# Hybrid pooling and chunked attention block: four half products between two attention tiles move into the heads, the sums of squares move from the heads to between the tiles

## The chip, the cores and the metric

The kernel runs on one core of one Trainium2 chip. The metric is the device time of one execution in microseconds (us), less is better; the times below are from three runs, with their median. Engines are named as the profile names them: PE is TensorE, which multiplies matrices, PEld its weight loads, DVE is VectorE, ACT is ScalarE, POOL is GpSimd, and SP is SyncE, which issues the DMAs.

## What is computed

One layer for 4096 rows of width 1024. The rows are normalised and projected to 3072 columns: a value and a gate for a pooling mixer, and q, k, v and a gate for attention with 8 heads of width 64. Attention goes by chunks of 64 rows; each chunk reads itself and the 8 chunks before it, with a bias by clipped distance. The core of the reference:

```python
def one_chunk(args):
    c, qb = args
    start = c * CHUNK
    kb = lax.dynamic_slice_in_dim(kp, start, BAND, axis=1)
    vb = lax.dynamic_slice_in_dim(vp, start, BAND, axis=1)
    s = jnp.einsum('bqhd,bkhd->bhqk', qb, kb).astype(jnp.float32) * scale + bias[None]
    valid = (start + j - pad) >= 0
    s = jnp.where(valid[None, None, None, :], s, MASK_VALUE)
    p = jax.nn.softmax(s, axis=-1)
    return jnp.einsum('bhqk,bkhd->bqhd', p.astype(vb.dtype), vb)
...
y_attn = chunked_rel_attention(qh, kh, vh, rel_bias[layer]) * jax.nn.silu(attn_g)
y = jnp.concatenate([y_pool, y_attn], axis=-1)
x = x + jnp.einsum('bse,ed->bsd', y, w_out[layer])
...
return rms_norm(x, final_norm_gain)
```

## The kernel before

Three stages follow one another: the normalised rows with the values and gates (until about 450 us), the pooling mixer with its share of the output (until about 890 us), and attention, which is what the change is in. Numbers that need more than 16 bits are kept as a high and a low f16 part.

Attention goes over 16 tiles `t` of 256 queries (`ATILES`, the last is `LAST`). Every engine has its own program, in the order in which it is written, and waits on semaphores. Each tile is a `boundary(t)` followed by `heads(t)`, eight heads `h`.

In the heads, PE makes the scores of head `h` in three groups `k` = 0, 1, 2 (`scores`, L1677 to L1685), in two banks that alternate; the scores two groups later may begin when the exponential has read the bank. Group 1 is the biased one: DVE adds the bias (`add_bias`, L1913) before ACT takes the exponential. ACT makes for each group the exponential (L1808) and its high half (L1814), POOL the low half (`p_lo`, L2029), and PE multiplies the values with both (`values(t, h - 1)`, L1705 to L1707), behind the scores of head `h`. Two heads ahead, PE makes the scores once more in the other layout (`maxima`, L1647, two per head, in one pair of banks) and DVE takes the row maximum with the bias (`maximum`, L1899); PE turns the maxima to rows (`max_rows`, L1659) and ACT copies them beside the queries (`max_row`, L1792). The next maxima wait for the DVE operation before them.

Meanwhile PE makes K and Q of tile `t + 1`, as seven products each by a scheme of the Strassen kind: K is w = 2t + 2, Q is w = 2t + 3. Each product is two halves of 12 matmuls (`kq_half`, L1489 to L1492), so a tile has 28 halves. Products 0 and 4 are copied by ACT (`kq_copy_p1` L1503, `kq_copy_c11` L1509), products 1, 2, 3, 5 and 6 are taken by DVE (`kq_take` 0 to 4, L1526). Product 0 of Q waits for all five takes of K. When K is complete, ACT makes its high half (`kq_hi`, L1534, at `K_HI_AT`) and POOL its low half (`kq_lo`, L1538, behind the `p_lo` of the head that `K_HI_AT` names). Take 2 of Q, of product 3, writes over the sums that `kq_lo` reads, and waits for it. DMAs from SP then move K and Q into place; the first maxima of a tile wait for them.

A table by hand, `KQ_SLOTS`, says how many halves stand in each head behind the scores of group 0 and of group 1; `KQ_BEFORE` says how many stand in `boundary`. The output product of tile `t - 1` (`output`, L1623) is in heads 6 and 7 and in the next boundary, its sum with the residual rows on DVE (`residual`, L1943). The mean of squares of the finished rows of tile `t - 2` is made by ACT (`square`, L1823), its root by POOL (`rstd`, L2037, L2039, in heads 1 and 2), and the rows are scaled by DVE (`finish`, L1952, at the end of heads 2 and 3).

## Time and profile before

| | us |
|---|---|
| median of three runs | 1805.46 |
| lowest and highest | 1803.0, 1809.53 |
| the profiled execution | 1807.35 |
| its span in the trace | 1805.6 |
| PE busy | 1644.2 (91%) |
| DVE busy | 1068.5 (59%) |
| ACT busy | 843.5 (47%) |
| POOL busy | 708.4 (39%) |

PE is the engine with the most work in every stage. Attention begins near 890 us and takes half of the span. The transposes that open a boundary start at 932.56 us for tile 1, 984.05 for tile 2, 1099.35 for tile 4, 1156.67 for tile 5 and 1733.90 for the last. A row of the timeline gives the start in us from the span's start, the duration, and in brackets how long the engine stood idle before it and what ended that. A duration of a single matmul includes its way through the array: what counts is the distance from one start to the next. A row of the windows gives the stretch, its length, then the busy us and the number of operations of PE, PEld, DVE, ACT and POOL, the clock that PE was granted as a share of 2.4 GHz, the busy share of the DMA engines and the GB/s that they moved.

### The profile page before, as it was taken

Reading aid. Unit: us, or ns where it says so; the run is one execution under the profiler, and the core shown is the slowest. Engines: PE = TensorE matmul, PEld = TensorE weight load, DVE = VectorE, ACT = ScalarE, POOL = GpSimd, SP = SyncE. Lnnn points to the kernel's source line nnn. Section 1 sums busy time; section 2 is a strip of 40 time slices with the busy share of each in tenths; the row PEclk is TensorE's granted clock in tenths of the full one; section 3 lists DMA queues with packets and bytes.
Section 4 is the critical chain, followed back from the end, with each engine's and each line's share of the span. In section 5 each row is a group of like instructions: output and inputs, shape, how many; then the busy total and the mean of one; then the engine's idle time right before and its main releaser. Section 6 shows DMA issues by size and latency. Waiting matters only on the chain. (4 is left out here: it accounts for less than half of the span.)

```text
span 1805.6 us, 43913 instructions
## 1 busy us (share of the span) xinstructions
PE 1644.2 (91%) x17920; PEld 1220.5 (68%) x17920; DVE 1068.5 (59%) x2188; ACT 843.5 (47%) x1580; POOL 708.4 (39%) x734
## 2 busy tenths in 40 slices
PE   5999699999999999999879999999999999999977
PEld 2554345568667676777567787778777787778854
DVE  7767477747456556544355565556655565556654
ACT  5554455422112111111145766567565765667565
POOL 3534345311112121001324644465545654456544
PEclk8999899999999999999989999999999999999999
DMA  5655574462542453244743342442334332442332
GB/s 205 209 204 200 196 247 170 170 251 72 186 164 83 163 187 129 83 159 166 218 147 101 99 131 79 136 131 106 102 106 148 112 125 72 136 148 90 107 94 83
DMA packets 111231, 257.84 MB, mean 143 GB/s; under 512 B 11928, under 2 KB 24744, under 8 KB 108984
## 3 DMA queue, kind: packets, MB, share of 16 engines
q1 hardware_dynamic: 109992, 253.73, 42.0%
q8 instruction: 143, 2.34, 0.5%
q0 software_dynamic: 1040, 1.31, 0.4%
q14 instruction: 56, 0.46, 0.1%
HBM read 151.33 MB, written 83.48 MB: 130 GB/s over the span
## 5 line engine op out<-in xcount | busy, mean ns | idle before, releaser
L2029 POOL TENSOR_TENSOR stages<-stages 128x512 f16<-128x512 f32 (+1 forms) x368 | 379.3, 1046 | 445.3 <-ACT stages L1814 445.1
L1489 PE MATMUL bank<-middle,weights 128*128 128x128 f16 x1792 | 315.0, 220 | 14.0 <-DVE middle L1526 13.1
L1492 PE MATMUL bank<-middle,weights 128*128 128x128 f16 x1792 | 314.6, 220 | 0.0
L1491 PE MATMUL bank<-middle,weights 128*128 128x128 f16 x1792 | 314.5, 220 | 0.0
L1808 ACT ACTIVATE stages<-bank,log_ps 128x512 f32<-128x512 f32 (+1 forms) x368 | 222.0, 603 | 163.9 <-POOL stages L2029 93.4
L1899 DVE CUSTOM_DVE_ANT_0 stages<-bank,stages 128x640 bf16<-128x640 f32 (+4 forms) x256 | 200.0, 781 | 158.2 <-PE bank L1647 157.9
L975 PE MATMUL bank<-middle 128*128 128x256 f16 x784 | 215.7, 275 | 7.5 <-DVE stages L1103 7.5
L977 PE MATMUL bank<-middle 128*128 128x256 f16 x784 | 215.7, 275 | 0.0
L978 PE MATMUL bank<-middle 128*128 128x256 f16 x784 | 215.6, 275 | 0.0
L1677 PE MATMUL bank<-middle 128*128 128x128 f16 (+1 forms) x840 | 169.4, 244 | 46.5 <-ACT stages L1808 41.9
L1814 ACT ACTIVATE stages<-stages 128x512 f16<-128x512 f32 (+1 forms) x368 | 203.5, 553 | 11.7
L288 PE MATMUL bank<-weights,middle 128*128 128x512 f16 x448 | 172.5, 385 | 25.9 <-DVE stages L584 15.9
L1489 PEld LDWEIGHTS bank<-middle,weights 128*128 128x128 f16 x1792 | 175.9, 98 | 17.5 <-DVE middle L1526 15.9
L1623 PE MATMUL bank<-entry,stages 128*128 128x512 f16 x768 | 181.1, 379 | 1.6 <-DVE stages L1876 1.0
L998 PE MATMUL bank<-entry,stages 128*128 128x512 f16 x768 | 171.6, 380 | 11.4 <-DVE entry L1195 11.4
L1491 PEld LDWEIGHTS bank<-middle,weights 128*128 128x128 f16 x1792 | 176.1, 98 | 0.4
L1492 PEld LDWEIGHTS bank<-middle,weights 128*128 128x128 f16 x1792 | 175.8, 98 | 0.0
L290 PE MATMUL bank<-weights,middle 128*128 128x512 f16 x448 | 172.2, 384 | 0.0
L291 PE MATMUL bank<-weights,middle 128*128 128x512 f16 x448 | 171.9, 384 | 0.0
L1262 POOL TENSOR_TENSOR stages<-stages 128x512 f16<-128x512 f32 x32 | 39.4, 1230 | 282.1 <-ACT stages L1051 282.1
L998 PEld LDWEIGHTS bank<-entry,stages 128*128 128x128 f16 x768 | 74.3, 98 | 101.2 <-DVE entry L1195 17.3
L1680 PE MATMUL bank<-middle 65*128 65x256 f16 x616 | 130.3, 242 | 0.0
(147 smaller groups left out, 3544.3 us busy)
## 6 DMA issues: line engine op xcount, KB each, us to landing
entry<-in_x SPq DMA_DIRECT2D x64, 512.0 KB, 3.6
h_ops<-middle SPq DMA_DIRECT2D x16, 1792.0 KB, 6.1
middle<-h_ops SPq DMA_DIRECT2D x112, 256.0 KB, 5.1
middle<-h_ops SPq DMA_DIRECT2D x49, 512.0 KB, 6.9
middle<-middle SPq DMA_DIRECT2D x192, 128.0 KB, 2.3
residual<-entry SPq DMA_DIRECT2D x32, 512.0 KB, 2.8
entry<-residual SPq DMA_DIRECT2D x30, 512.0 KB, 4.1
out<-entry SPq DMA_DIRECT2D x30, 512.0 KB, 2.9
```

The source lines that it names most:

```text
L975: nc.tensor.matmul(bank, wh, hop[:, :, s, 0, kt, :], start=(kt == 0 and s < 4), stop=False, skip_group_check=True)
L977: nc.tensor.matmul(bank, wh, hop[:, :, s, 1, kt, :], start=False, stop=False, skip_group_check=True)
L978: mm = nc.tensor.matmul(bank, wl, hop[:, :, s, 0, kt, :], start=False, stop=(kt == 3), skip_group_check=True)
L998: mm = nc.tensor.matmul(op[n2], part, w[:, kt, n2 * 512:(n2 + 1) * 512], start=(kt == 0 and w is wot_h and part is yh), stop=(kt == NKT - ...
L1489: nc.tensor.matmul(dst, wh, hop3[:, o, 0, kt, :], start=(kt == 0 and s < 2 and pair == 0), stop=False, skip_group_check=True)
L1491: nc.tensor.matmul(dst, wh, hop3[:, o, 1, kt, :], start=False, stop=False, skip_group_check=True)
L1492: mm = nc.tensor.matmul(dst, wl, hop3[:, o, 0, kt, :], start=False, stop=(kt == 3), skip_group_check=True)
L1623: mm = nc.tensor.matmul(bank[:, :], yh, w, start=(m == 0), stop=(m == 11))
L1808: nc.scalar.activation(p32[:, s, a:b], sta[s][:, a:b], ACT.Exp, bias=log_ps[:, 0:1]).then_inc(A["exp_done"], 1)
L1814: nc.scalar.activation(p_h[:, h % 2, c + a:c + b], p32[:, s, a:b], ACT.Copy).then_inc(A["ph_done"], 1)
L1899: nc.vector.tensor_tensor_reduce(junk2[:, c:640], wide[:, c:640], bias_q[:, h, c:640], 1.0, -3e38, ALU.add, ALU.max, m16[:, h % 2, j:j + 1 ...
L2029: nc.gpsimd.tensor_tensor(p_l[:, h % 2, c + a:c + b], p32[:, s, a:b], p_h[:, h % 2, c + a:c + b], ALU.subtract).then_inc(A["pl_done"], 1)
```

## The change

Four of the eight halves leave the boundary: one stands in front of each of the four maxima instead of two. The heads take them, one more in the second slot of heads 1 to 4, so that each slot of heads 0 to 5 holds one whole product. With that every product of K and the first six of Q end in another place, K's high half is made in head 3 instead of head 2, and its low half on POOL follows. DVE takes one product of K in the boundary instead of three. The two squares stand in ACT's boundary instead of behind heads 0 and 1.

```diff
-        KQ_BEFORE = 8
-        KQ_SLOTS = ((2, 2), (2, 1), (2, 1), (2, 1), (2, 1), (2, 2), (0, 0), (0, 0))
-        K_HI_AT, Q_HI_AT = (2, 0), (6, 0)
+        KQ_BEFORE = 4
+        KQ_SLOTS = ((2, 2), (2, 2), (2, 2), (2, 2), (2, 2), (2, 2), (0, 0), (0, 0))
+        K_HI_AT, Q_HI_AT = (3, 0), (6, 0)
...
-                steps(0, 2)
+                steps(0, 1)
                 maxima(t, 0, 0)
-                steps(2, 4)
+                steps(1, 2)
                 maxima(t, 0, 1)
-                steps(4, 6)
+                steps(2, 3)
                 max_rows(t, 0)
                 maxima(t, 1, 0)
-                steps(6, 8)
+                steps(3, 4)
                 maxima(t, 1, 1)
...
             def boundary(t):
+                if t > 1:
+                    square(t - 2, 0)
                 if t > 0:
                     for j in range(2):
                         branch_hi(t - 1, j)
                 if t < LAST:
                     kq_copy_p1(act, 2 * t + 2)
+                if t > 1:
+                    square(t - 2, 1)
                 max_row(t, 0)
...
-                    if t > 1 and h < 2:
-                        square(t - 2, h)
...
                 maximum(t, 0, 0)
+                maximum(t, 0, 1)
+                maximum(t, 1, 0)
                 take(0)
-                maximum(t, 0, 1)
-                take(1)
-                maximum(t, 1, 0)
-                take(2)
                 maximum(t, 1, 1)
```

The first place is DVE's program at the start of a middle tile, from the low halves of the transposes to the biased scores of head 0. `ISA` is the maximum, L1526 a take, L1913 (L1915 in the changed file) the biased scores. Before:

```order
1554 L1876 SCALAR_TENSOR_TENSOR stages<-bank,stages 128x4x128 [waits a_yth_done] x2
1555 L1899 ISA stages,m<-bank,stages 128x640 [waits a_mrow_mm,a_max_done,a_max_mm]
1556 L1899 ISA m 128x1
1557 L1526 SCALAR_TENSOR_TENSOR middle<-bank,middle 128x256 [waits a_kq_u,a_kq_p,a_kq_mm]
1558 L1899 ISA stages,m<-bank,stages 128x640 [waits a_max_done,a_max_mm]
...
1560 L1526 SCALAR_TENSOR_TENSOR middle<-bank,middle 128x256 [waits a_kq_u,a_kq_mm]
...
1563 L1526 SCALAR_TENSOR_TENSOR middle<-bank,middle 128x2x128 [waits a_nat_lo,a_kq_u,a_kq_mm]
...
1566 L1899 ISA stages,m<-bank,stages 128x640 [waits a_mrow_mm,a_max_done,a_max_mm]
1567 L1899 ISA m 128x1
1568 L1913 TENSOR_TENSOR bank<-bank,stages 128x512 [waits a_st_mm]
```

The same stretch of the changed kernel:

```order
1554 L1878 SCALAR_TENSOR_TENSOR stages<-bank,stages 128x4x128 [waits a_yth_done] x2
1555 L1901 ISA stages,m<-bank,stages 128x640 [waits a_mrow_mm,a_max_done,a_max_mm]
...
1559 L1901 ISA stages,m<-bank,stages 128x640 [waits a_mrow_mm,a_max_done,a_max_mm]
1560 L1901 ISA m 128x1
1561 L1526 SCALAR_TENSOR_TENSOR middle<-bank,middle 128x256 [waits a_kq_u,a_kq_p,a_kq_mm]
1562 L1901 ISA stages,m<-bank,stages 128x640 [waits a_max_done,a_max_mm]
...
1564 L1901 ISA stages,m<-bank,stages 128x640 [waits a_mrow_mm,a_max_done,a_max_mm]
1565 L1901 ISA m 128x1
1566 L1526 SCALAR_TENSOR_TENSOR middle<-bank,middle 128x256 [waits a_kq_u,a_kq_mm]
1567 L1915 TENSOR_TENSOR bank<-bank,stages 128x512 [waits a_st_mm]
```

Of the three takes among the four maxima one is left, ahead of the last, and a take now stands between head 2's first maximum and the biased scores of head 0.

The second place is POOL's program from head 1 to head 4 of a middle tile. L2029 is `p_lo` (three in each head), L2037 and L2039 are `rstd`, L1538 is `kq_lo`. Before:

```order
263 L2029 TENSOR_TENSOR stages<-stages 128x512 [waits a_ph_done] x2
264 L2029 TENSOR_TENSOR stages<-stages 128x256 [waits a_ph_done]
265 L2037 TENSOR_TENSOR stat<-stat,eps 128x1 [waits a_fin_done,a_ss_done]
266 L2039 TENSOR_TENSOR stat<-stat,pow_half 128x1 [waits a_ms_done]
267 L1538 TENSOR_TENSOR middle<-middle 128x1024 [waits a_nat_hi]
268 L2029 TENSOR_TENSOR stages<-stages 128x512 [waits a_ph_done] x2
269 L2029 TENSOR_TENSOR stages<-stages 128x256 [waits a_ph_done]
```

The same stretch of the changed kernel:

```order
263 L2029 TENSOR_TENSOR stages<-stages 128x512 [waits a_ph_done] x2
264 L2029 TENSOR_TENSOR stages<-stages 128x256 [waits a_ph_done]
265 L2037 TENSOR_TENSOR stat<-stat,eps 128x1 [waits a_fin_done,a_ss_done]
266 L2039 TENSOR_TENSOR stat<-stat,pow_half 128x1 [waits a_ms_done]
267 L2029 TENSOR_TENSOR stages<-stages 128x512 [waits a_ph_done] x2
268 L2029 TENSOR_TENSOR stages<-stages 128x256 [waits a_ph_done]
269 L1538 TENSOR_TENSOR middle<-middle 128x1024 [waits a_nat_hi]
```

`kq_lo` has moved behind the three `p_lo` of head 3.

## Rows read from the trace of the kernel before

**Rows 1.** Windows, tile 4, first maxima to head 6: busy us (operations) of each engine.
```profile
1102.17:1107.40 5.23, 5.23 (x89) 5.16 (x90) 3.30 (x9) 0.38 (x1) 0.00 (x0) 1.00 0.43 151
1107.40:1112.00 4.60, 4.60 (x75) 4.28 (x73) 2.68 (x7) 2.79 (x6) 1.16 (x1) 1.00 0.01 4
1112.00:1117.70 5.70, 4.89 (x91) 4.62 (x91) 3.63 (x9) 5.48 (x11) 3.03 (x4) 1.00 0.00 0
1117.70:1123.17 5.47, 4.89 (x97) 4.67 (x93) 3.39 (x11) 5.30 (x11) 3.58 (x5) 1.00 0.01 3
1123.17:1128.47 5.30, 4.88 (x91) 4.66 (x91) 4.52 (x11) 3.80 (x8) 4.54 (x5) 1.00 0.27 104
1128.47:1135.18 6.71, 5.06 (x90) 4.63 (x91) 5.00 (x11) 3.91 (x8) 5.84 (x5) 1.00 0.56 184
1135.18:1140.56 5.38, 5.38 (x102) 5.28 (x103) 3.02 (x9) 4.51 (x9) 3.01 (x4) 1.00 0.99 346
```

**Rows 2.** Waits of PE in tiles 3 to 14: us, times, longest us.
```profile
PE bank L1677 <- ACT stages L1808: 34.5, 60, 1.3
...
PE bank L1647 <- DMA middle<-middle: 7.3, 9, 1.3
```

**Rows 3.** Timeline of PE in head 1 of tile 4, the first product of Q.
```profile
1113.91 0.44 PE L1647 MATMUL bank<-middle 128*128 128x256 f16 x3
...
1115.62 0.23 PE L1489 MATMUL bank<-middle,weights 128*128 128x128 f16 x1 [0.81 <-DVE middle L1526]
```

**Rows 4.** Timeline of PE between tiles 3 and 4: start, duration, operation, idle before.
```profile
1102.17 0.43 PE L1647 MATMUL bank<-middle 128*128 128x256 f16 x3 [0.44 <-DVE stages L1876]
...
1105.78 0.22 PE L1489 MATMUL bank<-middle,weights 128*128 128x128 f16 x1
...
1107.12 0.44 PE L1647 MATMUL bank<-middle 128*128 128x128 f16 x4
1107.40 0.22 PE L1677 MATMUL bank<-middle 128*128 128x128 f16 x1
```

**Rows 5.** Timeline of PE in tile 15, head 1, where no products stand between maxima.
```profile
1747.40 0.43 PE L1647 MATMUL bank<-middle 128*128 128x256 f16 x3
...
1748.77 0.45 PE L1647 MATMUL bank<-middle 128*128 128x128 f16 x4 [0.29 <-DVE m L1899]
```

**Rows 6.** Timelines of DVE, ACT and PE in head 3 of tile 4.
```profile
1126.31 0.42 DVE L1526 SCALAR_TENSOR_TENSOR middle<-bank,middle 128x256 f32<-128x256 f32 x1
1126.64 0.69 DVE L1913 TENSOR_TENSOR bank<-bank,stages 128x512 f32<-128x512 f32 x1
...
1127.72 0.69 ACT L1808 ACTIVATE stages<-bank,log_ps 128x512 f32<-128x512 f32 x1
1128.44 0.63 ACT L1814 ACTIVATE stages<-stages 128x512 f16<-128x512 f32 x1
...
1128.47 0.23 PE L1677 MATMUL bank<-middle 128*128 128x128 f16 x1 [0.42 <-ACT stages L1808]
```

**Rows 7.** Timeline of ACT in tile 15, the square behind head 0.
```profile
1748.15 1.04 ACT L1823 ACTIVATE middle<-entry 128x1024 bf16<-128x1024 f32 x1
```

**Rows 8.** Timelines of POOL and DVE in heads 3 and 4 of tile 4.
```profile
1127.22 2.13 POOL L1538 TENSOR_TENSOR middle<-middle 128x1024 f16<-128x1024 f32 x1
1128.68 1.76 DVE L1952 SCALAR_TENSOR_TENSOR entry<-entry,stat 128x1024 f32<-128x1024 f32 x1
1129.32 2.13 POOL L2029 TENSOR_TENSOR stages<-stages 128x512 f16<-128x512 f32 x1
...
1131.42 1.15 POOL L2029 TENSOR_TENSOR stages<-stages 128x512 f16<-128x512 f32 x1
...
1132.55 0.67 POOL L2029 TENSOR_TENSOR stages<-stages 128x256 f16<-128x256 f32 x1
```

**Rows 9.** Windows at the start of tile 15: the first holds its first maxima.
```profile
1735.00:1739.20 4.20, 0.89 (x7) 0.49 (x7) 2.19 (x5) 0.63 (x2) 0.00 (x0) 1.00 0.93 266
1739.30:1746.10 6.80, 4.99 (x32) 3.55 (x33) 3.88 (x9) 2.09 (x5) 1.15 (x1) 0.50 0.51 190
```

## What is predicted

> **What bounds the kernel now.** I read the windows by head first [rows 1]. They cut tile 4 of the attention stage (the one whose transposes start at 1099.35 us) at the first matmul of each head. The reader is to see that PE is busy for most of every stretch (5.23 of 5.23 between the tiles, 4.60 of 4.60, then 4.89 of 5.70, 4.89 of 5.47, 4.88 of 5.30, 5.06 of 6.71, 5.38 of 5.38) and that what it lacks lies in heads 1 to 4. The 13 tiles 2 to 14 have this pattern, each 57.3 to 58.2 us long, so they carry the result. Next, who ends PE's waits over twelve of them [rows 2]: ScalarE's exponentials, 34.5 us in 60 waits, or 2.9 us per tile; then there are the DMAs that move queries and keys, 7.3 in 9; and once per tile a product waits for a take of VectorE (0.81 us in tile 4 [rows 3]). PE's number of matmuls does not change, so the time can only change by how long it stands still. I therefore follow the starts of its groups from the first maxima of the tile, which waits for VectorE or a DMA and not for products, so it keeps its place.
>
> **Between the tiles.** A half product takes 0.67 us: two took 1105.78 to 1107.12 [rows 4]. A pair of halves and the maxima took 1.61 us, and four maxima with their products ran from 1102.17 to the first scores at 1107.40, 5.23 us. With one half in each gap PE has only 0.28 + 0.67 = 0.95 us of work from one maxima to the next, and the maxima wait for VectorE: where that loop is bare, the next ones start 1.37 us later (1747.40 to 1748.77) [rows 5]. So: maxima at 0, 1.37; the max rows at 2.74; maxima at 2.85 (two short matmuls for the max rows, 0.11 at 24 in 1.34 us) and 2.85 + 1.37 = 4.22; scores 0.28 later, at 4.50. That is **0.73 us less, where 2.67 us of matmuls were taken out**: the rest of the room becomes a wait. The moved take of VectorE (0.33 us of its queue [rows 6]) comes after half 4 at 3.80 + 0.2 and before the last maximum at 4.70; it is covered by that loop. The first square (1.04 us [rows 7]) goes into ScalarE's idle time before the transposes. The second starts after the copy of product 1, near 1.55, and ends near 2.6; the max rows come to ScalarE at about 3.06, so it costs nothing. It would cost up to 1.04 us if the max rows were an early event.
>
> **Head 0** keeps four halves, but they are now products 2 and 3: the first ends in a take ahead of the biased scores in VectorE's queue, where there was a copy on ScalarE. A take ahead of them moves them by 0.33 us (1126.31 to 1126.64 [rows 6]). They set the exponential and that sets the next head's scores. 4.60 + 0.33 = 4.93.
>
> **Heads 1 to 3.** A head with four halves whose only limit is PE lasts 5.38 us, as head 5 shows [rows 1]. Head 1 becomes one (was 5.70): its wait at 1115.62, 0.81 us after the half before it, has gone to head 2. That wait comes where the first product of Q needs all five takes of K: the last take stands behind a maximum, and the chain from the maxima to the product was 1113.91 to 1115.62, 1.71 us [rows 3]. Head 2 now gets what head 1 had, two halves, that wait and one half, and a second half behind it: 5.70 + 0.67 = 6.37 (was 5.47). Head 3 is at PE's limit, 5.38 (was 5.30). The squares' 2 x 1.04 us leave ScalarE, but only the two waits of heads 2 and 3 went with them, and 2 x 0.67 us of matmuls take their place.
>
> **Head 4** is the term that decides. K's low half on POOL (kq_lo, 2.13 us) moves behind the three p_lo of head 3 instead of head 2. VectorE's third take of Q in head 4 waits for it, and behind that take, in order, stand the biased scores of head 4, their exponential, and head 5's scores. From the start of head 3: the biased scores at 3.47 (1126.64 - 1123.17), 0.70, exponential and copy 0.03 + 0.69 + 0.03 + 0.63 = 5.55 [rows 6]. POOL's p_lo 5.63 to 6.78 (1.15 [rows 8]). VectorE's finish (L1952) is asked for 0.8 into head 4, at 6.18, so it stands against that p_lo. The rows of before show what they do to each other: the finish, whose record is 1.76 us long, was held until the end of kq_lo (1127.22 + 2.13 = 1129.35), ended 1.09 us after it at 1130.44, and the next p_lo took 2.13 instead of 1.15 [rows 8]. Here the finish ends at 6.78 + 1.08 = 7.86, the short p_lo (0.67 alone) about 0.52 later at 8.38, kq_lo at 10.48. Then take 10.53, biased scores 10.86, and 0.70 + 0.03 + 0.69 + 0.05 to head 5's scores: 12.33, less head 3's 5.38 is 6.95 (was 6.71).
>
> The tie between POOL and VectorE at 6.78 is the unknown. If VectorE had not to be waited for, kq_lo would end 1.0 us sooner and head 4 last 5.97; if POOL went on first and the finish ran after kq_lo, the maximum and the take behind the finish would come at about 5.3 and 6.05 us of head 4 and the head end near 7.85. I take 6.95, since the one row of that kind has VectorE go between. The Trainium skill (SBUF — State Buffer, under "Reading the diagram" of its first part) says that whichever operation starts first holds the pair of ports that the two share for the whole instruction, a VectorE operation with two inputs in SBUF among them; the row agrees (2.13 for 1.15), and by that rule too the waiting finish would go first.
>
> **From head 5 on** nothing moves: the last product of Q ends in the same slot, its high and low halves and the moves of K and Q start as before, and the loads for the tile after next wait for products that end no later than head 5.
>
> **The sum of a middle tile**: 4.50 + 4.93 + 5.38 + 6.37 + 5.38 + 6.95 = 33.51 us against 33.01 before, +0.50; x 13 = +6.5 us. The other three are estimates. Tile 0: the loop between tiles is shorter there and its heads have idle PE, -2.0 (from 0 to -3). Tile 1: boundary -1.0, but it has little idle time in heads 1 to 4 and gets the same two waits, +1.5 (0 to +2). Tile 15 has no products; ScalarE fills its heads 1 and 2, so the square of 1.04 us [rows 7] gives back part of itself at each, -0.9 (0 to -2.1). Against the profiled execution's own span of 1805.6 us (1807.35 in all) that is +5.1, and +1 for the clock, below: 1811.7. The median of the runs shown, 1805.46, lies 1.9 us below that execution, so the same change, +6.1, gives **1811.6**.
>
> **Rivals.**
> *A, faster:* head 4 has no collision, because POOL gets both p_lo and kq_lo through before the finish matters. Each middle tile is then 0.98 us shorter than in my sum, -0.48 against before; 13 x -0.48 - 1.4 = -7.6, 1798. The sign turns at a head 4 of 6.95 - 0.50 + 1.4 / 13 = 6.56 us. For it: 6.95 rests on one pattern of records. Against it: the finish of before met POOL in the same place [rows 8].
> *B, POOL first:* +0.9 per middle tile more, 1811.6 + 12 = 1823. Against it, the row.
> *C, the waits fill:* the added halves lie in the 2.9 us of waits for ScalarE and nothing new appears: 13 x 2.9 = 38, 1768. This is what the change would do if ScalarE were the limit of the heads because of the squares. Against it: 1.65 of them are in head 4 (6.71 - 5.06 [rows 1]), where POOL was last (the p_lo held up behind the finish [rows 8]), and the loop of the maxima is in the way between the tiles.
> *D, the clock falls between the tiles.* PE will stand still for 1.1 us or more before the first maxima (0.44 before, up to 1.28, plus one half of 0.67), then about 0.3 us in each of three loops. In tile 15, where it was busy for 0.89 of 4.20 us, the granted clock went from 1.00 to 0.50, that is from 2.4 to 1.2 GHz, for the next 6.8 us, and in the heads of before it stayed at 1.00 with 5.06 of 6.71 busy [rows 1, 9]. The new boundary lies between: near 60% where the moves are in time, near 40% where a DMA is late, as in 9 of 12 tiles [rows 2]. A fall there costs up to 1.7 us; I put one such fall (half hidden, +1) into the sum; at six or more it gives 1819. The Trainium skill (TensorE: Matmul & The Clock Gate, "What's actually happening") says that half rate is the state at rest and that activity releases it; by that, every late boundary could pay, 9 x 1.7 = 15 us; the trace shows it only for a much emptier stretch.
> *E, the special tiles and the overlap give more than I grant*: nothing measurable, 1803 to 1808.
>
> **How the numbers follow.** My forecast (1807 to 1815) 45%, A 15%, B 7%, C 4%, D 15%, E 14%. The measurement can tell about 0.3% from nothing, 5.4 us, so 1800.0 and 1810.9 are the bounds. The forecast lies astride the upper one: of its 45, 25 are slower and 20 the same. Slower: 25 + 7 + 14 = 46%. Same: 20 + 14 + 3 of A + 1 of D = 38%. Faster: 12 + 4 = 16%. The range leaves out C, most of B and about a third of A: 1798.5 to 1820.
>
> **What would show it.** First maxima to first scores of a middle tile near 4.5 us with PE idle three times for a maximum; head 0 near 4.93; head 1 without a wait, head 2 near 6.37 with a wait of about 0.8 for a take; head 4 near 6.95, VectorE's take there waiting for POOL, and kq_lo starting about 1 us after the p_lo before it would have been done. If head 4 is near 6.0, A holds; if PE's clock is below 1.00 in head 0 of several tiles, D. A sum is wrong at the root if the first maxima of a tile move against the last scores before it, for then a DMA, not this order, has changed.

## The result

| | before | changed |
|---|---|---|
| median, us (four runs each) | 1806.38 | 1820.14 |
| lowest and highest | 1803.0, 1809.53 | 1817.97, 1821.44 |
| profiled execution, and its span | 1807.35, 1805.6 | 1817.97, 1816.2 |

The changed kernel takes 1.0075 of the time before, 95% interval [1.0054, 1.0097]: it is slower by 0.75%. The direction was forecast, the size was not: +6.1 us were predicted and the medians differ by 13.8. The range ended at 1820, on a before of 1805.46; 1.0075 times that is 1819.0, at its upper end (the median itself, 1820.14, is measured beside 1806.38). Measured a second time (run e11), the same kernel took 1821.59 beside 1811.19, 1.0058 [1.0035, 1.0082].

The head of the page of the changed kernel, with the span and the busy time of each engine:

```profile
span 1816.2 us, 43913 instructions
PE 1650.0 (91%) x17920; PEld 1225.6 (67%) x17920; DVE 1065.6 (59%) x2188; ACT 841.5 (46%) x1580; POOL 706.5 (39%) x734
```

Nothing in it tells of a change: PE's share is still 91%. It has to be read head by head. The windows of tile 4, cut as in [rows 1]:

```profile
1102.19:1106.71 4.52, 3.73 (x52) 3.15 (x53) 2.84 (x7) 1.79 (x4) 0.00 (x0) 1.00 0.50 174
1106.71:1111.64 4.93, 4.64 (x75) 4.29 (x72) 3.08 (x7) 2.39 (x5) 1.15 (x1) 1.00 0.00 0
1111.64:1117.03 5.39, 5.38 (x102) 5.29 (x103) 3.06 (x9) 4.73 (x10) 2.94 (x3) 1.00 0.01 3
1117.03:1123.40 6.37, 5.56 (x108) 5.29 (x105) 3.47 (x10) 4.52 (x10) 4.37 (x6) 1.00 0.01 3
1123.40:1128.78 5.38, 5.38 (x108) 5.28 (x105) 4.57 (x11) 4.17 (x7) 3.85 (x5) 1.00 0.26 98
1128.78:1135.83 7.05, 5.56 (x108) 5.33 (x104) 5.00 (x12) 3.35 (x8) 5.98 (x4) 1.00 0.51 177
1135.83:1141.21 5.38, 5.38 (x102) 5.28 (x103) 3.21 (x10) 4.50 (x9) 2.94 (x3) 1.00 1.01 352
```

Line by line against [rows 1]: 4.52 for 5.23, 4.93 for 4.60, 5.39 for 5.70, 6.37 for 5.47, 5.38 for 5.30, 7.05 for 6.71, 5.38 for 5.38, together 33.64 for 33.01 without the last, +0.63. From head 5 on a middle tile is 0.02 shorter, so the whole tile is +0.60. Forecast were 4.50, 4.93, 5.38, 6.37, 5.38, 6.95, 5.38. PE is the limit in heads 1 and 3 (5.38 busy), and stands still between the tiles, in head 2 and in head 4.

Between the tiles the timeline of PE shows the bare loop: maxima, a wait for the maximum on VectorE (L1901), and the next maxima.

```profile
1102.19 0.43 PE L1647 MATMUL bank<-middle 128*128 128x256 f16 x3 [1.10 <-DVE stages L1878]
...
1103.56 0.45 PE L1647 MATMUL bank<-middle 128*128 128x128 f16 x4 [0.26 <-DVE m L1901]
...
1104.94 0.28 PE L1659 MATMUL bank<-ident,m 128*128 128x128 f16 x2 [0.26 <-DVE m L1901]
1105.06 0.44 PE L1647 MATMUL bank<-middle 128*128 128x256 f16 x3
...
1106.43 0.45 PE L1647 MATMUL bank<-middle 128*128 128x128 f16 x4 [0.26 <-DVE m L1901]
```

The steps are 1.37, 1.38 and, from 1105.06, 1.37 us: the 1.37 of [rows 5] with no products, although one half product of 0.67 us stands in each. Four halves of 0.67 us left, and 0.71 us came of it.

The wait for the take is in head 2 now; head 4 follows it, as DVE, POOL and PE show it:

```profile
1120.65 0.23 PE L1489 MATMUL bank<-middle,weights 128*128 128x128 f16 x1 [0.81 <-DVE middle L1526]
...
1129.59 1.68 DVE L1954 SCALAR_TENSOR_TENSOR entry<-entry,stat 128x1024 f32<-128x1024 f32 x1
1130.14 1.65 POOL L2029 TENSOR_TENSOR stages<-stages 128x256 f16<-128x256 f32 x1
1131.77 2.12 POOL L1538 TENSOR_TENSOR middle<-middle 128x1024 f16<-128x1024 f32 x1
1134.03 0.42 DVE L1526 SCALAR_TENSOR_TENSOR middle<-bank,middle 128x256 f32<-128x256 f32 x1 [2.02 <-POOL middle L1538]
1134.37 0.69 DVE L1915 TENSOR_TENSOR bank<-bank,stages 128x512 f32<-128x512 f32 x1
...
1135.84 0.23 PE L1677 MATMUL bank<-middle 128*128 128x128 f16 x1 [1.50 <-ACT stages L1808]
```

The short p_lo, 0.67 us in [rows 8], takes 1.65 beside the finish (L1954); only then does kq_lo (L1538) begin, the take waits 2.02 us for it, and the biased scores (L1915), an exponential and PE's 1.50 us follow. By the Trainium skill (SBUF — State Buffer, "Reading the diagram") whichever of two such operations starts first keeps the ports for the whole instruction; the rows agree, in both orders, as experiment e4 shows below. Which of the two goes on when one waits already is not in that rule; in each of the 13 middle tiles here the waiting finish went ahead of POOL's next p_lo, as forecast.

Who ended PE's waits in tiles 3 to 14 (us, times, longest us):

```profile
PE bank L1677 <- ACT stages L1808: 24.1, 36, 1.5
PE bank L1647 <- DMA middle<-middle: 13.6, 8, 2.2
...
PE bank L1647 <- DVE m L1901: 5.7, 22, 0.3
```

ScalarE's 34.5 us in 60 waits [rows 2] became 24.1 in 36, 10.4 us less. That isn't a gain: the added products stand where those waits were, so PE needs the room itself; and 13.6 us for DMAs (7.3 before) and 5.7 for the maxima stand beside them.

**Where the 10.6 us of span are.** From transposes to transposes. Tile 1's began 2.0 us earlier (932.56 to 930.60), tile 1 took 0.5 more. Tiles 2 to 14 went from 749.85 to 760.21 us, +10.36: 13 x 0.60 for the order = 7.8; two boundaries at a lower clock, 0.8 each = 1.6; and the first maxima began 0.96 us later in all (40.57 to 41.53 us after their transposes, summed). Tile 15 and the end, +1.8. The sum is +10.6. The medians differ by 3 us more than that because of the executions that were profiled: the changed kernel's is the fastest of its four (2.2 us below their median), that of before is 1.0 above its own.

The 2.0 us at the start are not tile 0's. PE's matmuls are in the same order in both kernels until just before tile 0's first maxima, and in the changed kernel's execution they were ahead by 2.25 us already when the last output products ahead of attention began (863.70 and 861.45 us). From there to tile 1's transposes it took 0.3 us more, not less.

**Only the middle tiles repeat.** In the second profiled execution of the changed kernel (e11) tiles 2 to 14 took 760.14 us (760.21 here). All else moved: tile 1's transposes began at 933.63, tile 1 took 53.80 us (51.95 here), tile 15 51.51 (53.09 here, 51.32 in before). Against before, that is +1.1, +2.3, +10.3 and +0.2, +13.8 in all. So some 10.3 us lie in the middle tiles in both, of which 7.8 are the order's, and the rest differs as much between two executions of one kernel as between the two kernels.

### The profile page after: what moved, and what is told of

Read it like the earlier page. It is cut to its first block and busy times, and to the rows that moved or that the text cites. A ratio compares the mean times of both kernels' runs of the same rounds, so it can differ in the third digit from the quotient of the medians.

```text
span 1816.2 us, 43913 instructions
## 1 busy us (share of the span) xinstructions
PE 1650.0 (91%) x17920; PEld 1225.6 (67%) x17920; DVE 1065.6 (59%) x2188; ACT 841.5 (46%) x1580; POOL 706.5 (39%) x734
## 5 line engine op out<-in xcount | busy, mean ns | idle before, releaser
L2029 POOL TENSOR_TENSOR stages<-stages 128x512 f16<-128x512 f32 (+1 forms) x368 | 368.9, 1017 | 456.5 <-ACT stages L1814 454.9
L1901 DVE CUSTOM_DVE_ANT_0 stages<-bank,stages 128x640 bf16<-128x640 f32 (+4 forms) x256 | 200.0, 781 | 188.8 <-PE bank L1647 188.4
L1677 PE MATMUL bank<-middle 128*128 128x128 f16 (+1 forms) x840 | 171.0, 246 | 31.8 <-ACT stages L1808 27.7
L1647 PE MATMUL bank<-middle 128*128 128x128 f16 (+1 forms) x848 | 111.8, 247 | 37.9 <-DMA middle<-middle 21.0
```

The lines of the kernel that those rows point to most:

```text
L1901: nc.vector.tensor_tensor_reduce(junk2[:, c:640], wide[:, c:640], bias_q[:, h, c:640], 1.0, -3e38, ALU.add, ALU.max, m16[:, h % 2, j:j + 1 ...
L2029: nc.gpsimd.tensor_tensor(p_l[:, h % 2, c + a:c + b], p32[:, s, a:b], p_h[:, h % 2, c + a:c + b], ALU.subtract).then_inc(A["pl_done"], 1)
```

## The experiments

Tile 4, or its like, from first maxima on, and the sum of tiles 2 to 14 of each profiled execution. Heads 0 and 1 stand together, since their border (the first scores, or the first that wait) differs among the kernels by 0.35 us and their sum doesn't.

| kernel | boundary | heads 0+1 | 2 | 3 | 4 | 5 | 6 | tiles 2 to 14 |
|---|---|---|---|---|---|---|---|---|
| before | 5.23 | 10.30 | 5.47 | 5.30 | 6.71 | 5.38 | 5.10 | 749.85 |
| changed | 4.52 | 10.32 | 6.37 | 5.38 | 7.05 | 5.38 | 5.09 | 760.21 |
| e1 | 5.23 | 10.30 | 5.04 | 5.37 | 6.71 | 5.38 | 5.09 | 745.31 |
| e2 | 4.52 | 10.32 | 6.37 | 5.38 | 7.05 | 5.38 | 5.10 | 760.17 |
| e3 | 4.52 | 10.32 | 6.38 | 5.37 | 5.39 | 5.37 | 5.09 | 738.64 |
| e4 | 4.53 | 10.32 | 6.37 | 5.38 | 6.07 | 5.38 | 5.51 | 750.37 |
| e5 | 5.23 | 10.30 | 5.45 | 5.87 | 5.06 | 5.38 | 5.09 | 737.41 |
| e6 | 5.23 | 10.30 | 5.04 | 5.87 | 5.06 | 5.38 | 5.09 | 732.08 |
| e7 | 4.52 | 10.32 | 5.39 | 5.37 | 6.00 | 5.38 | 5.10 | 734.45 |
| e8 | 5.23 | 9.32 | 5.70 | 5.87 | 5.06 | 5.38 | 5.09 | 726.19 |
| e9 | 4.52 | 10.32 | 6.37 | 5.38 | 7.05 | 5.38 | 5.09 | 762.40 |
| e10 | 5.23 | 9.32 | 5.70 | 4.94 | 5.48 | 5.38 | 5.21 | 722.16 |
| e11 | 4.52 | 10.32 | 6.37 | 5.38 | 7.05 | 5.38 | 5.10 | 760.14 |
| e12 | 4.52 | 10.32 | 5.39 | 5.38 | 5.48 | 5.38 | 5.53 | 732.54 |

Kernels were measured beside their own runs of before, at 1806.7 to 1811.2 us, so ratios are what compares. e11 is the changed kernel once more. Two theories stood at the start. By the first, the halves cost what the prediction says, the squares nearly nothing, and head 4 is set by kq_lo behind the p_lo and the finish. By the second, the squares in ScalarE's boundary do the harm, or kq_lo's place does none.

### One part at a time: e1 and e2

e1 is before with the squares alone between the tiles; e2 is the changed kernel with the squares back in the heads.

```diff
+                if t > 1:
+                    square(t - 2, 0)
...
+                if t > 1:
+                    square(t - 2, 1)
...
-                    if t > 1 and h < 2:
-                        square(t - 2, h)
```

> The kernel before with the two squares moved between the tiles and nothing else. Theory 1 (VectorE's wait for the low half of K in head 4 and the wait for the last take set the middle tile, the squares only lengthen head 2): head 2 falls from 5.47 to about 4.97 us, heads 3 and 4 keep the chain through POOL within 0.1 us, so about -0.4 us per middle tile, -5 us over 13, and about -1 us in the last tile: near 1800 us where before is 1806. Theory 2 (the squares between the tiles delay the max rows, and that is where the changed kernel lost its time): first maxima to first scores grows from 5.23 us by up to 1.04 us per tile, and the kernel is 5 to 13 us slower than before.

> The changed kernel with its two squares put back behind heads 0 and 1: only the half products are moved. Theory 1: the middle tile is that of the changed kernel, head for head (4.52, 4.93, 5.39, 6.37, 5.38, 7.05 us), since ScalarE has 0.2 us or more to spare in heads 1 and 2 with the squares too, so the ratio to before is near 1.007; only the last tile differs, by 1 to 2 us. Theory 2 (the squares cost the time): it is 5 us or more faster than the changed kernel, ratio near 1.002 or below.

e1 took 1802.04 us beside 1806.86, 0.9972 [0.9959, 0.9984]; e2 1822.48, 1.0086 [1.0065, 1.0106]. The windows of e1, boundary and head 2:

```profile
1101.88:1107.11 5.23, 5.23 (x88) 5.16 (x89) 3.29 (x9) 1.40 (x3) 0.00 (x0) 1.00 0.45 160
...
1117.41:1122.45 5.04, 4.89 (x96) 4.66 (x92) 3.30 (x10) 4.36 (x9) 3.58 (x5) 1.00 0.02 3
```

The boundary is 5.23 as before: the squares delay nothing there. Head 2 is 5.04 for 5.47, since its exponential no longer stands behind a square. So the squares' move is a gain of 0.3%, and the second theory fell. In e2 every head of a middle tile is that of the changed kernel, squares or not: with the halves in the heads, the 0.43 us that the squares cost head 2 are hidden by PE's own work and its wait for the take. The two parts of the change don't add up: the gain of the one is used up by the other, and the whole loss is the halves'.

### kq_lo behind the first p_lo: e3, e5 and e6

```diff
                     nc.gpsimd.tensor_tensor(p_l[:, h % 2, c + a:c + b], p32[:, s, a:b], p_h[:, h % 2, c + a:c + b],
                                             ALU.subtract).then_inc(A["pl_done"], 1)
+                    if k == 0 and t < LAST and h == K_HI_AT[0]:
+                        kq_lo(pool, 2 * t + 2)
...
-                    if t < LAST and h == K_HI_AT[0]:
-                        kq_lo(pool, 2 * t + 2)
```

kq_lo now stands behind the first p_lo of its head and ahead of the other two. e3 makes this edit in the changed kernel, e5 in before, e6 in e1.

> The changed kernel with the low half of K on POOL behind the first p_lo of head 3 instead of the third. Theory 1 (head 4 waits in the order POOL low half, VectorE take, biased scores, exponential): kq_lo ends about 2 us into the end of head 3's own work, head 4 falls from 7.05 to 5.4 us (PE's limit), everything else stays, 13 x -1.65 = -21 us: near 1799 us where before is 1806, ratio 0.995 to 0.997. Rival (head 4 is long for another reason: the exponential waits for p_lo, or the finish on VectorE): head 4 falls by 0.5 us at most, and the ratio stays above 1.003.

> The kernel before with the low half of K on POOL behind the first p_lo of head 2 instead of the third. It asks whether the same order was also the price in the kernel before. Theory 1 (POOL's late kq_lo holds up head 4 of before): heads 3 and 4 together fall from 12.0 to about 10.7 us, with head 3 longer (5.8, its exponentials wait for the p_lo behind kq_lo) and head 4 near 5.0; 13 x -1.3 = -17 us, ratio near 0.990. Rival (in before nothing but the finish on VectorE matters there): heads 3 and 4 together stay within 0.3 us of 12.0, ratio 0.998 or more.

> The kernel before with the squares between the tiles and the low half of K behind the first p_lo of head 2. Theory 1: head 2 as in the run with the squares alone (5.04), heads 3 and 4 near 5.8 and 4.9 instead of 5.38 and 6.71, 13 x -1.4 = -18 us against that run, 1784 us, ratio near 0.987. Rival (the two gains are the same one): no faster than the run with the low half alone.

e3 took 1794.17 us, 0.9934 [0.9911, 0.9958]; e5 1794.48 beside 1808.32, 0.9921 [0.9902, 0.9939]; e6 1788.77, 0.9897 [0.9881, 0.9914]. Head 4 of e3:

```profile
1123.18:1128.57 5.39, 5.39 (x109) 5.29 (x105) 5.25 (x11) 3.44 (x8) 4.48 (x4) 1.00 0.32 109
```

PE is busy for all of it: 1.66 us are gone with one line moved, and all waits of head 4 with it. This is the cause of head 4's 7.05, shown. In e5, heads 3 and 4:

```profile
1120.59:1126.46 5.87, 5.05 (x90) 4.66 (x91) 5.15 (x12) 3.79 (x8) 5.67 (x6) 1.00 0.24 94
1126.46:1131.52 5.06, 4.89 (x90) 4.67 (x90) 4.08 (x10) 3.79 (x8) 3.55 (x4) 1.00 0.55 189
```

Head 4 drops from 6.71 to 5.06, head 3 pays 0.57 of it, and 0.8% stays. The cost was in the kernel before as well, in the same head 4, though kq_lo stood a head earlier there. e3 against e6, which has the squares between the tiles too, says what the halves in the heads cost once kq_lo is out of the way: 738.64 for 732.08 in the middle tiles, 0.5 us a tile.

### The finish one head later: e4

```diff
-                    if t > 1 and h in (2, 3):
-                        finish(t - 2, h - 2)
+                    if t > 1 and h in (2, 3 if t == LAST else 4):
+                        finish(t - 2, int(h > 2))
```

> The changed kernel with the second finish of the output on VectorE behind head 4 instead of head 3 (the last tile keeps it in head 3, since its DMAs wait for it). It takes away the meeting of finish and p_lo ahead of the low half of K. Theory 1: kq_lo starts about 1.0 us sooner, head 4 falls from 7.05 to about 6.05 us and head 5 stays at 5.38, 13 x -1.0 = -13 us: near 1807, ratio near 1.000. Rival (the two engines do not hold each other up, the records are only long): head 4 stays within 0.3 us of 7.05 and the ratio near 1.007.

1810.55 us, 1.0018 [1.0005, 1.0031]. Head 4, and at the end of it what the finish now meets:

```profile
1131.20:1137.27 6.07, 5.55 (x108) 5.33 (x104) 3.49 (x11) 3.35 (x8) 5.00 (x4) 1.00 0.01 4
```

```profile
1137.74 1.27 DVE L1954 SCALAR_TENSOR_TENSOR entry<-entry,stat 128x1024 f32<-128x1024 f32 x1
1137.96 2.70 POOL L2029 TENSOR_TENSOR stages<-stages 128x512 f16<-128x512 f32 x2 [1.52 <-ACT stages L1814]
```

Head 4 is 6.07 for 7.05, as expected: 0.98 of it was the collision, the number that rival A was priced with. Here the finish began first: it takes 1.27 us, and POOL's two p_lo 2.70 where they take 1.79 unhindered (1115.24 in e8). Head 6 grew from 5.09 to 5.51, which I had not expected. The reason is ScalarE's chain there. Its rows in heads 5 and 6 of e12, whose head 6 grew alike:

```profile
1136.27 0.69 ACT L1808 ACTIVATE stages<-bank,log_ps 128x512 f32<-128x512 f32 x1 [0.96 <-DVE bank L1915]
...
1138.95 0.69 ACT L1808 ACTIVATE stages<-bank,log_ps 128x512 f32<-128x512 f32 x1 [0.52 <-POOL stages L2032]
...
1140.72 1.06 ACT L1534 ACTIVATE middle<-middle 128x1024 f16<-128x1024 f32 x1
1141.80 0.69 ACT L1808 ACTIVATE stages<-bank,log_ps 128x512 f32<-128x512 f32 x1
```

From head 5's biased exponential to head 6's are 5.53 us, a wait for POOL and Q's high half (L1534, 1.06) among them. In the changed kernel the same two stand 1140.03 to 1145.56, also 5.53. But there the first begins 4.19 us into head 5, in e12 4.64 us into it, behind maxima and takes that the later finish has pushed back; that PE is late by the difference is what head 6 shows. In e4 itself it is 4.62 us into it, and 5.53 from the one to the other (1141.89 to 1147.42).

### The take ahead of the maximum: e7 and e8

The wait for the take (0.81 us) comes where the last take of K stands behind a maximum. e7 is e3, and e8 is e6, with that take in front:

```diff
+                        steps = kq_steps(slot(h, k)) if t < LAST else []
+                        if (0, 6) in steps:
+                            kq_take(dve, 2 * t + 2, KQ_TAKES[6])
                         if h + 2 < HEADS:
                             maximum(t, h + 2, k)
-                        if t < LAST:
-                            for w, s in kq_steps(slot(h, k)):
-                                if s in KQ_TAKES:
-                                    kq_take(dve, 2 * t + 2 + w, KQ_TAKES[s])
+                        for w, s in steps:
+                            if s in KQ_TAKES and (w, s) != (0, 6):
+                                kq_take(dve, 2 * t + 2 + w, KQ_TAKES[s])
```

> The changed kernel with the low half of K behind the first p_lo of head 3, and VectorE's last take of K ahead of the maximum instead of behind it. Theory 1 (Q's first product waits in head 2 for that take because a maximum of 0.75 us stands before it, which itself waits for PE): the wait in head 2 goes, head 2 falls from 6.37 to about 5.4 us, 13 x -1.0 = -13 us against the run with the low half alone (1794): near 1781, ratio 0.986. Rival (the wait is the take's own latency, or the maximum that is now later holds the biased scores): head 2 stays above 6.0.

> The kernel before, eight half products between the tiles as there, with the squares between the tiles, the low half of K behind the first p_lo of head 2 and the last take of K ahead of the maximum. Theory 1: head 1 loses its wait of 1.0 us too, 13 x -0.95 = -12 us against the kernel without the take: near 1772 us, ratio 0.981, and faster than the changed kernel with the same two repairs (1781), because between the tiles PE loses nothing to the loop of the maxima. Rival (moving the halves is worth something once the waits of the heads are gone): the changed kernel with the two repairs is as fast or faster.

e7 took 1790.48 us, 0.9902 [0.9885, 0.9919], nine more than expected; e8 1785.18, 0.9876 [0.9858, 0.9893], thirteen more. Both takes did what they should, and both gains were lost again in part. Heads 2 and 4 of e7, and what happened in head 4:

```profile
1113.94:1119.33 5.39, 5.39 (x108) 5.29 (x105) 3.52 (x10) 3.91 (x9) 3.75 (x6) 1.00 0.01 3
...
1124.70:1130.70 6.00, 5.56 (x108) 5.33 (x104) 5.33 (x13) 3.35 (x8) 5.11 (x4) 1.00 0.46 166
```

```profile
1125.51 1.57 DVE L1954 SCALAR_TENSOR_TENSOR entry<-entry,stat 128x1024 f32<-128x1024 f32 x1
1125.94 2.15 POOL L2031 TENSOR_TENSOR stages<-stages 128x512 f16<-128x512 f32 x1
1128.19 0.69 ACT L1808 ACTIVATE stages<-bank,log_ps 128x512 f32<-128x512 f32 x1 [2.51 <-POOL stages L2031]
```

Head 2 fell from 6.37 to 5.39 and head 4 rose from 5.39 to 6.00: the finish, a microsecond earlier than in e3, now meets kq_lo, the next p_lo takes 2.15, and the exponential waits 2.51 us for it. Three boundaries at a lower clock in e7, where e3 had one, cost another 1.6 us. In e8, heads 0 and 1 fell from 10.30 to 9.32 and head 2 rose from 5.04 to 5.70. ScalarE's rows say why:

```profile
1113.82 0.69 ACT L1808 ACTIVATE stages<-bank,log_ps 128x512 f32<-128x512 f32 x1 [0.19 <-DVE bank L1915]
...
1116.50 0.69 ACT L1808 ACTIVATE stages<-bank,log_ps 128x512 f32<-128x512 f32 x1 [0.52 <-POOL stages L2033]
...
1118.27 1.06 ACT L1534 ACTIVATE middle<-middle 128x1024 f16<-128x1024 f32 x1
...
1119.63 0.68 ACT L1808 ACTIVATE stages<-bank,log_ps 128x512 f32<-128x512 f32 x1
```

From biased exponential to biased exponential it is 5.81 us, with the wait for POOL and K's high half in it: PE had been late enough before to hide this chain. Both forecasts missed for one reason above all: I took a wait out and did not ask what was next late, the question on which the prediction had rested.

### Two halves first between the tiles: e9

The changed kernel had its clock lowered in two boundaries. e9 puts two of the four halves ahead of the first maxima, one ahead of the second and none ahead of the third:

```diff
-                steps(0, 1)
+                steps(0, 2)
                 maxima(t, 0, 0)
-                steps(1, 2)
+                steps(2, 3)
                 maxima(t, 0, 1)
-                steps(2, 3)
                 max_rows(t, 0)
```

> The changed kernel with the same four halves between the tiles, placed 2, 1, 0, 1 in front of the four maxima instead of 1, 1, 1, 1. The first maxima do not wait for products, so first maxima to first scores stays 4.52 us and every head stays; only where PE stands still moves: 0.44 to 1.3 us before the first maxima instead of 1.1 to 2.2. Theory 1 with the clock as a part of its own (a late DMA on top of 1.1 us of idle time makes the granted clock fall, 0.8 us each): no boundary of 5.3 us in tiles 2 to 14 any more, and 1 to 3 us less than the changed kernel beside it. Rival (the clock falls for another reason, such as the loops after the first maxima): boundaries of 5.3 us are still there in one to three of the 13 tiles, time as the changed kernel.

1821.33 us beside 1811.19, 1.0052 [1.0033, 1.0071]: nothing gained, and my expectation fell. Two boundaries still had the lower clock, and one of them reached into head 0:

```profile
1217.46:1220.86 3.40, 2.08 (x32) 1.92 (x30) 1.88 (x3) 2.37 (x5) 0.00 (x0) 1.00 0.54 106
1220.86:1226.14 5.28, 4.09 (x41) 3.52 (x41) 2.80 (x7) 0.51 (x3) 0.00 (x0) 0.75 0.52 189
1226.14:1231.14 5.00, 5.00 (x74) 4.62 (x72) 2.90 (x8) 2.11 (x4) 1.16 (x1) 0.92 0.01 3
```

The third number from the right is the granted clock (1.00, 0.75, 0.92). PE had more to do before the first maxima, 2.08 us busy in 3.40, and it fell all the same; in both tiles the maxima were late, 3.70 and 3.68 us after the transposes where 2.81 is the least.

### Finish after head 3, and the changed kernel with every repair: e10, e11 and e12

e10 is e8 with both finishes a head later in the middle tiles; e12 is e7 with the same edit; e11 is the changed kernel once more.

```diff
-                    if t > 1 and h in (2, 3):
-                        finish(t - 2, h - 2)
+                    first = 2 if t == LAST else 3
+                    if t > 1 and h in (first, first + 1):
+                        finish(t - 2, h - first)
```

> The kernel with all three repairs on the old placing of the halves (1785), with the two finishes behind heads 3 and 4 instead of 2 and 3 in all tiles but the last. Theory 1 (head 3 is 5.87 us there because the first finish waits for kq_lo and then holds up p_lo): head 3 falls to about 4.9 us, head 4 grows by up to 0.4, 13 x -0.5 = -7 us or better: near 1778. Rival (head 3 is long because p_lo stands behind kq_lo itself): head 3 stays above 5.6 us and the time at 1785 or above.

> The changed kernel as it is, beside the run with the halves placed 2, 1, 0, 1 on the same chip. Theory 1: its middle tile again head for head (4.52, 4.93, 5.39, 6.37, 5.38, 7.05), ratio to before near 1.008, and one to three boundaries of 5.3 us in tiles whose moves land late. Rival (the first measurement was an outlier, and +0.60 us per middle tile is all): ratio 1.005 or less.

> The changed kernel with the low half of K first, the last take of K first, and the finishes behind heads 3 and 4: the same repairs as in the fastest kernel so far, so that the two differ in the placing of the half products alone. Theory 1 (the loop of the maxima wastes what the heads gain): heads 2 to 4 at 5.4 us each, PE's limit, first maxima to first scores 4.52, the middle tile near 55.6 us in all where the fastest kernel has 55.1, so 13 x 0.5 = 6 us slower, near 1786 and ratio 0.986 to before. Rival (the placing pays once the heads' waits are gone): ratio 0.982 or below, no slower than the fastest kernel.

e10 took 1779.72 us, 0.9824 [0.9808, 0.9839], the fastest of all; e11 1821.59, 1.0058 [1.0035, 1.0082], its middle tile again head for head and one boundary at a lower clock; e12 1788.43 beside 1806.73, 0.9893 [0.9876, 0.991]. Heads 3 and 4 of e10:

```profile
1116.22:1121.16 4.94, 4.88 (x90) 4.66 (x90) 3.00 (x9) 3.79 (x8) 4.75 (x6) 1.00 0.02 5
1121.16:1126.64 5.48, 5.01 (x90) 4.67 (x90) 4.73 (x13) 3.80 (x8) 3.92 (x4) 1.00 0.25 99
```

Head 3 gives 0.93 us and head 4 takes 0.42 of it back. e12 against e10 is the fairest test of where the halves should stand, with kq_lo, take and finish in good places in both: 55.83 against 55.10 us in the undisturbed tile, and 732.54 against 722.16 in all thirteen. By the rows of the table: -0.71 between the tiles, +1.00 in heads 0 and 1, -0.31 in head 2, +0.44 in head 3, +0.32 in head 6. The four halves cost 9.5 us (13 x 0.73) there, although no wait is left in heads 1 to 3: heads filled to 5.38 by PE alone replace heads that other engines let end earlier. I had expected 0.5 us a tile; head 6 is what I had left out.

## Why the prediction was right in sign and short in size

**What held.** The sum of a middle tile: +0.50 forecast, +0.60 measured, with six of seven terms within 0.02 us, in both profiled executions of the changed kernel. The room between the tiles became a wait for VectorE (4.50 forecast, 4.52). The take moved the biased scores of head 0 (4.93). The wait for the take went to head 2 with its 0.81 us (6.37). The squares between the tiles cost nothing, and their leaving gave nothing beside the halves (e1, e2). Head 4 was held by kq_lo behind the p_lo behind the finish (e3, e4).

**Head 4**, 6.95 forecast, 7.05 measured: from kq_lo's end to the take I put 0.05 us, and it is 0.14 (1131.77 + 2.12 = 1133.89 to 1134.03). Over 13 tiles the 0.1 is 1.3 us.

**The clock**, +1 forecast. Two of 13 boundaries paid 0.8 each, where I had one fall at +1, of up to 1.7. No row of before gave that 1.7. The window from tile 5's first maxima on, against 4.52 at 1.00 in tile 4:

```profile
1157.84:1161.24 3.40, 1.17 (x17) 1.02 (x16) 1.65 (x3) 1.08 (x2) 0.00 (x0) 1.00 0.86 194
1161.24:1166.56 5.32, 5.01 (x52) 4.40 (x53) 2.84 (x7) 1.79 (x4) 0.00 (x0) 0.68 0.51 181
```

PE was busy for 1.17 of 3.40 us, at 1.00, and the boundary behind it had 0.68 as its mean, between the levels 2.4 and 1.2 GHz. The fall costs only 0.8 us here, where PE waits for VectorE for part of the loop anyway. In tile 1 of e1 the lower clock reached into a boundary with all eight halves, in which PE is busy throughout; that took 1.7 us more than the 4.90 of before:

```profile
937.09:943.71 6.62, 6.62 (x85) 6.47 (x85) 2.62 (x9) 0.38 (x1) 0.00 (x0) 0.73 0.82 305
```

The mechanism of rival D is there, with a third of the boundaries that D needed. The Trainium skill (TensorE: Matmul & The Clock Gate, "What's actually happening") has activity as what releases the half rate, by which I had put every late boundary, nine of them, at risk: two of 13 fell here, so this trace agrees with the direction and not with that reading of it.

**Tile 15**, -0.9 forecast, +1.8 in this pair of executions, is the term furthest off. From its transposes to head 1, heads 1 and 2, and heads 3 and 4, in the kernel before:

```profile
1733.90:1746.80 12.90, 7.21 (x49) 4.84 (x47) 7.52 (x15) 3.84 (x7) 1.15 (x1) 0.74 0.64 204
1746.80:1756.50 9.70, 6.79 (x108) 5.24 (x108) 5.59 (x17) 9.44 (x18) 6.46 (x8) 1.00 0.01 3
1756.50:1766.90 10.40, 8.66 (x119) 6.36 (x120) 7.75 (x17) 7.83 (x16) 7.94 (x9) 1.00 0.41 152
```

And in the changed one:

```profile
1742.76:1756.45 13.69, 7.87 (x49) 5.04 (x48) 7.53 (x15) 4.89 (x10) 1.15 (x1) 0.61 0.62 193
1756.45:1765.65 9.20, 8.64 (x108) 7.55 (x109) 5.39 (x15) 7.67 (x15) 6.58 (x8) 0.65 0.01 3
1765.65:1777.57 11.92, 9.86 (x126) 7.53 (x123) 8.83 (x18) 8.22 (x16) 8.57 (x9) 0.86 0.37 135
```

The squares' leaving did shorten heads 1 and 2 (9.70 to 9.20, even at a mean clock of 0.65). But the clock was low for longer at the start, 0.61 for 0.74 (+0.8), and fell a second time in the heads, where it had been 1.00: +1.5 in heads 3 and 4. I had looked for clock falls between the tiles and not in the heads of the one tile that has no products to fill PE. But two executions of one kernel differ in this as much: the second execution of the same kernel (e11) has

```profile
1747.57:1799.08 51.51, 40.34 (x490) 29.24 (x488) 30.25 (x73) 32.44 (x60) 26.24 (x28) 0.87 0.29 94
```

for the whole tile, where this one has 53.09 and before 51.32. Tile 15 has one order in all the kernels here but for the squares. Without squares in its heads it took 50.2 to 53.1 us, 51.5 in the mean of 11 profiled executions, with them 51.3 to 52.3, 52.0 in the mean of three (before, e2, e5). The gain of 0.9 that I forecast is neither shown nor refuted by that, and the clock fell again in its heads in 4 of the 11 and in none of the three. Whether the squares' place has to do with it stays open: three are too few.

**Terms that were right by luck or not in the sum.** Up to tile 1's transposes I had -2.0 for tile 0, and -2.0 is what the times say; but 2.25 of it came ahead of the change, and tile 0 itself gave +0.3. Its reason (a shorter loop, idle PE in its heads) is not borne out. Tile 1 took +0.5 where I had +1.5, and 2.3 more than before in e11. The first maxima of the middle tiles began 0.96 us later in all, mostly behind DMAs; their sum is 40.6 to 42.6 us in the six kernels with eight halves between the tiles and 40.5 to 42.8 in the eight executions with four, so this is not shown to be an effect of the change either. So of +10.6: 7.8 + 1.6 + 0.96 - 2.0 + 0.5 + 1.8, where I had 6.5 + 1 + 0 - 2.0 + 1.5 - 0.9 = 6.1. The difference of 4.5 is tile 15 by 2.7, head 4 by 1.3, the first maxima by 1.0, the clock by 0.6, and tile 1 by 1.0 the other way. What repeats in both executions is the middle tiles, 10.4 and 10.3 us for 7.5 forecast. Head 4's 1.3 is in both; the rest is the late first maxima (0.96 and 1.5), for which I had nothing, and the clock (1.6 and 0.8 for 1), which vary from execution to execution.

**What stays open**: the size of the change within about 3 us. The medians differ by 13.8 in the first measurement and by 10.4 (1821.59 less 1811.19) in the second, the profiled executions by 10.6 and 13.8.

**Rivals.** A and B fell on the tie between POOL and VectorE: the finish went between the two p_lo in each middle tile. C fell: of 13 x 2.9 us of waits for ScalarE 10.4 went, and no time came of it, for PE's limit of 5.38 and the loop between the tiles stand under those waits. E fell. D was there in small; its 1819 for six falls was a sum of its own, since six at 1.7 would be 1820.8 and six at 0.8 give 1815.4.

## What to carry to other kernels

Work moved off the gaps of a full engine frees only what the next loop leaves: here four halves of 0.67 us gave 0.71 us, since the maxima and VectorE need 1.37 us a turn with one half between them or none. Follow one tile through every engine's queue, and once a wait is taken out, ask what is late next before its gain is counted; both times that this was left out (e7, e8), about two thirds of a middle tile's gain were lost again. And look first at the one long operation that stands in a helper engine's queue behind short urgent ones: a line that moved kq_lo ahead of two of the three p_lo was worth 0.8%, and with the squares, the take and the finish 1.8%, more than the balance of the work between heads and boundary, which cost 0.75%.

## What the runs showed of the hardware

**The clock fell only behind late first maxima, and not behind all of them.** Of the boundaries of tiles 2 to 14, none of 78 has a granted clock below 1.00 in the six kernels with eight halves there, and 13 of 104 have in the eight executions with four. All 13 had their first maxima 3.42 us or more behind the transposes; of the 104, 33 were as late, and none of the other 71 lost the clock. With eight halves 17 were as late, up to 4.13 us, and all kept it. So lateness was there each time and does not decide alone: first maxima 4.00 us behind the transposes (e11, tile 5) kept 1.00.

**Either engine holds the other up, nearly for the whole of an operation.** Behind kq_lo or a p_lo the finish waits and ends 1.08 to 1.09 us after it (1.27 is its time alone), and where the finish is first, POOL's p_lo of 1.15 us alone ends 1.01 us after the finish, with a record of 1.77 to 2.18 us. I had priced both from one row of each; what I had not followed up is where they meet next once a wait is gone, which e7 shows as 2.51 us of idle ScalarE.
